# First products begun on half their input, and an expert stage whose weight slots join in another order, with a sixth in layer 1

## Chip, core and metric

One NeuronCore of a Trainium2 chip runs the whole program; all tensors are float32. The metric is device time in microseconds (us), the median over runs. A profiled execution is a separate run of the same kernel whose trace is read here.

## What is computed

Two transformer blocks in sequence over 256 latent tokens with 1024 channels, beside 256 context tokens. The first block has two layers. Each layer is a mixer and an expert feed-forward:

```
h = modulate(rms_norm(x));  z = h @ w_in                  # 256 latent + 256 context rows
y = gated sum of (fourier mix, global attention, window attention) @ w_out
x = x + g1 * y
h = modulate(rms_norm(x));  aff = softmax(h @ w_router)   # 16 experts
top_aff, top_idx = top_k(aff.T, 32)                       # each expert takes its 32 tokens
a, u = h[top_idx] @ w_gate_e, h[top_idx] @ w_up_e         # per expert, 1024 x 1024 each
x = x + g2 * scatter_add((silu(a) * u) @ w_down_e * top_aff)
```

In layer 0 latent and context tokens both go through the experts (64 rows per expert), in layer 1 the latent tokens alone (32 rows). The experts' matrices are 3 x 4 MB for each of 16 experts, 201 MB a layer. The second block has one layer: a hybrid mixer (gated linear attention and a state-space part), then a dense SwiGLU feed-forward of width 2816.

## The kernel before

Five engine programs are written by hand and kept in order by counting semaphores. Each engine waits for its signals in program order, so what stands behind a waiting instruction waits too. `due(name, n)` adds n to an engine's own count of a semaphore and returns the value to wait for.

**Weights** come through a ring of `RING = 4` slots of 16 KB per partition (2 MB each). One load fills one slot: half of a 1024 x 1024 expert matrix, or 512 columns of another one. The sync engine's program (SP) issues all loads in the order in which TensorE will use them. `Slots` (L118) gives both programs the same turn: `take` hands out the slot at the head of the list and puts it at the end. `load` (L1843) waits until the former holder of its slot was read: `release` counts whole jobs, and `release_half` signals when the first half of a matrix was read.

In the expert stage a fifth slot, number `RING`, joins. It lies in the SBUF area `arena` at 12288, where layer-wide tables (`pick`, `pick_g`) stand earlier in the layer, so its first load waits for `picks_turned`, the job number behind the last transposed pick (L1779, L1850).

**Order of the expert stage's loads**, numbered from 0: gate and up of expert 0, first halves (0, 1), second halves (2, 3); then for each expert e the four of expert e+1, and the two halves of down e (so 4 to 7 belong to expert 1, 8 and 9 to down 0). There are 96. With `slots.add(RING)` the fifth slot is appended behind the four of the ring: load 4 goes into it, and every later load n takes the slot of load n-5.

**Order of TensorE's work in the expert stage** (`experts`, L1689): router logits and their turns, places, then `gather` (L1598): for each of 8 k, products of `xn2` and the one-hot `pick` that collect the chosen rows as columns of `xgT`. VectorE modulates and copies the even k (L2339), ScalarE the odd ones (L2704). Then `turn_picks` (transposes for the later scatter, copied by VectorE, L2348), a wait for `xg_ready` (L2343, behind `xgT_done` of ScalarE, L2738), then `gate_up(0, 0)`, `gate_up(0, 1)`. `gate_up(e, half)` (L1724) is 32 products of 512 columns over four k. `turn_hidden`, `down` and, every fourth expert, `scatter` follow.

**PSUM** is two pools of four banks: pool D is read by VectorE, pool A by ScalarE. `bank(pool)` waits for the bank's reader of four jobs ago.

**First products.** Four places start with normalised rows `xn` that TensorE transposes (`turn_half`, L1419) and VectorE (even k) and ScalarE (odd k) modulate into `hT`, four k at a time with a signal each, `hT_ready_dve` (L2222) and `hT_ready_act` (L2653). They are the two mixers of the first block, the second block, and its feed-forward. TensorE waits for both signals of each engine (`wait_stream`, L1431; also L400 and L642) ahead of the first product that reads them. A product over the inner dimension runs through k = 0 to 7.

**Start of the program** (L1811 to L1831): the modulation steps `mod_step` (products with `w_ada`, L1370; turned by L1386) stand between transposes of `xn` for both streams.

## Time and profile before

| what | us |
|---|---|
| runs | 2429.85 median of 3 (2420.85, 2429.85, 2430.94) |
| the profiled execution's own time | 2430.49 |
| its span, first to last instruction | 2428.7 |
| TensorE busy | 2152.5 (89%) |
| VectorE busy | 689.0 (28%) |
| ScalarE busy | 390.6 (16%) |
| mean granted TensorE clock | 0.937 |
| bytes read | 589 MB, 243 GB/s over the span |

The stages of the first block: layer 0's experts run from about 573 to 1090 us of the span, layer 1's from about 1399 to 1905 us; in between stand the mixers; the second block runs from 1918 us to the end. The own time is 1.8 us longer than the span. A product of 512 float32 columns shows as two records.

### The profile page before, as it was taken

The numbers are of one execution on the slowest core, as the hardware profiler recorded it, in microseconds if no ns is written. First come the engines' busy times: TensorE is split into PE (matmuls) and PEld (weight loads), VectorE is DVE, ScalarE is ACT, GpSimd is POOL, SyncE is SP. The second block draws the span as 40 slices with busy tenths as digits, with TensorE's granted clock in tenths as the row PEclk, the third lists the DMA queues.
The fourth block names the chain that finished last, engine by engine and source line by source line (L and its number), as shares of the span: only waits on it lengthen the run. The fifth ranks groups of instructions, "written<-read, shape, count | busy, mean of one in ns | idle before, by whom it ended". The sixth has DMA issues, their size and how long they took to land.

```text
span 2428.7 us, 21162 instructions
## 1 busy us (share of the span) xinstructions
PE 2152.5 (89%) x8446; PEld 1021.1 (42%) x8446; DVE 689.0 (28%) x1642; ACT 390.6 (16%) x811; POOL 0.2 (0%) x4
## 2 busy tenths in 40 slices
PE   6989999998889898989899967888888798989998
PEld 3445444444323332324544432222222345648873
DVE  2266111045112121223631231121111358740001
ACT  2045100012100000002430110010000214441000
POOL 0000000000000000000000000000000000000000
PEclk8999899999989998989999989899999999889999
DMA  9139523111799999992384339999999620113442
GB/s 352 69 113 364 209 87 95 69 69 70 320 428 428 429 429 426 429 415 85 134 329 143 139 158 422 429 429 429 429 425 429 234 80 25 70 62 112 148 156 78
DMA packets 106411, 591.62 MB, mean 244 GB/s; under 512 B 8151, under 2 KB 12071, under 8 KB 81611
## 3 DMA queue, kind: packets, MB, share of 16 engines
q1 hardware_dynamic: 102720, 585.34, 59.9%
q10 hardware_dynamic: 3595, 4.95, 0.6%
q8 instruction: 67, 1.10, 0.2%
q14 instruction: 29, 0.24, 0.0%
HBM read 589.22 MB, written 1.05 MB: 243 GB/s over the span
## 4 chain that ended last, share of the span: by engine, by line
PE 73%; DMA 17%; DVE 5%; ACT 2%; issue 2%; DVEq 0%; SPq 0%; ACTq 0%
PE bank L1404 23%; PE bank L1733 18%; DMA weight_ring<-in_w_up_e 13%; PE bank L654 6%; PE bank L1353 4%; PE bank L408 3%; PE bank L673 3%; PE bank L1760 3%; PE bank L1370 3%; DMA arena<-in_w_up_e 2%; DMA weight_ring<-in_w_ada 2%; PE bank L1604 2%; PE bank L1721 2%; PE bank L1682 1%; PE bank L469 1%
## 5 line engine op out<-in xcount | busy, mean ns | idle before, releaser
L1733 PE MATMUL bank<-weight_ring,arena 128*64 128x512 f32 (+1 forms) x1664 | 504.0, 652 | 113.0 <-DMA weight_ring<-in_w_up_e 89.5
L1404 PE MATMUL bank<-weight_ring,arena 128*128 128x512 f32 (+1 forms) x1360 | 581.6, 590 | 6.8 <-DVE small L2222 4.1
L1404 PEld LDWEIGHTS bank<-weight_ring,arena 128*128 128x128 f32 x1360 | 261.0, 193 | 322.0 <-issue 310.3
L1733 PEld LDWEIGHTS bank<-weight_ring,arena 128*64 128x64 f32 (+1 forms) x1664 | 146.1, 134 | 378.5 <-issue 372.9
L1733 PE MATMUL bank<-arena 128*64 128x512 f32 (+1 forms) x384 | 185.6, 640 | 19.8 <-DMA weight_ring<-in_w_up_e 15.3
L1760 PE MATMUL bank<-weight_ring,arena 128*64 128x512 f32 (+1 forms) x800 | 177.9, 593 | 0.4 <-DMA weight_ring<-in_w_down_e 0.4
L1353 PE MATMUL bank<-const,arena 128*128 128x128 f32 (+4 forms) x808 | 121.8, 305 | 62.9 <-DVE arena L2075 10.2
L2745 ACT ACTIVATE arena<-bank 64x512 f32<-64x512 f32 (+1 forms) x64 | 37.7, 589 | 768.0 <-PE bank L1733 767.8
L654 PE MATMUL bank<-arena,weight_ring 128*128 128x256 f32 x704 | 153.9, 382 | 2.2 <-DVE small L2222 2.2
L1353 PEld LDWEIGHTS bank<-const,arena 128*128 128x128 f32 (+4 forms) x808 | 106.3, 178 | 114.3 <-issue 65.8
L654 PEld LDWEIGHTS bank<-arena,weight_ring 128*128 128x128 f32 x704 | 134.9, 192 | 21.1 <-DVE small L2222 2.5
L2428 DVE TENSOR_TENSOR arena<-bank,arena 32x512 f32<-32x512 f32 x96 | 65.8, 686 | 183.2 <-PE bank L1760 181.0
L2413 DVE COPY arena<-bank 128x512 f32<-128x512 f32 (+1 forms) x32 | 17.9, 558 | 339.9 <-PE bank L1353 339.8
L2404 DVE TENSOR_TENSOR arena<-bank,arena 64x512 f32<-64x512 f32 (+1 forms) x64 | 44.1, 689 | 230.4 <-ACT arena L2745 229.0
L1760 PEld LDWEIGHTS bank<-weight_ring,arena 128*64 128x64 f32 (+1 forms) x800 | 53.9, 123 | 118.9 <-issue 113.7
L1370 PE MATMUL bank<-weight_ring,silu_c 128*32 128x512 f32 x576 | 73.2, 654 | 15.8 <-DMA weight_ring<-in_w_ada 15.8
L1733 PEld LDWEIGHTS bank<-arena 128*64 128x64 f32 (+1 forms) x384 | 48.8, 132 | 78.4 <-issue 72.0
L408 PE MATMUL bank<-arena,weight_ring 128*128 128x512 f32 (+3 forms) x192 | 76.1, 558 | 1.8 <-DVE small L2222 1.8
L673 PE MATMUL bank<-weight_ring,arena 128*128 128x512 f32 x176 | 75.8, 593 | 1.1 <-DVE arena L1102 1.1
L2155 DVE TENSOR_TENSOR arena<-bank,arena 128x512 f32<-128x512 f32 x24 | 16.6, 692 | 192.5 <-PE bank L1404 192.5
L2630 ACT ACTIVATE arena<-bank 128x512 f32<-128x512 f32 x36 | 21.5, 597 | 274.8 <-PE bank L1404 274.8
L1760 PE MATMUL bank<-arena 128*64 128x512 f32 (+1 forms) x224 | 52.4, 610 | 4.5 <-DVE arena L2413 4.0
(368 smaller groups left out, 1569.2 us busy)
## 6 DMA issues: line engine op xcount, KB each, us to landing
weight_ring<-in_w_gate_e SPq DMA_DIRECT2D x52, 2048.0 KB, 15.4
weight_ring<-in_w_up_e SPq DMA_DIRECT2D x52, 2048.0 KB, 12.3
weight_ring<-in_w_down_e SPq DMA_DIRECT2D x50, 2048.0 KB, 12.6
weight_ring<-in_w_ada SPq DMA_DIRECT2D x24, 2048.0 KB, 12.2
weight_ring<-in_w_in SPq DMA_DIRECT2D x23, 2048.0 KB, 9.9
arena<-in_w_down_e SPq DMA_DIRECT2D x14, 2048.0 KB, 14.6
arena<-in_w_gate_e SPq DMA_DIRECT2D x12, 2048.0 KB, 15.7
arena<-in_w_up_e SPq DMA_DIRECT2D x12, 2048.0 KB, 14.8
```

The source lines that it names most:

```text
L408: mm = pe.matmul(b[0:m, 0:n], slot_view(r)[:, k, c0:c0 + m], hT[:, k, 0:n], start=(k == 0), stop=(k == KD - 1))
L654: mm = pe.matmul(b[:, n * SEQ:n * SEQ + SEQ], slot_view(r)[:, k, blk * P:blk * P + P], h3T[:, k, :], start=(k == 0), stop=(k == KD - 1))
L673: mm = pe.matmul(bs[t][:, :], ffT[:, k, t * P:t * P + P], slot_view(r)[:, k - k0, :], start=(k == 0), stop=(k == FB - 1))
L1353: return pe.transpose(dst, src, ident[0:src.shape[0], 0:src.shape[0]])
L1370: mm = pe.matmul(b[at:at + 32, :], silu_pad[:, col:col + 32], wide(r)[:, k, n * 512:n * 512 + 512], start=(k == 0), stop=(k == KH - 1))
L1404: mm = pe.matmul(b[:, 0:c1 - c0], lhs[:, k, t * P:t * P + P], slot_view(r)[:, k, c0:c1], start=(k == 0), stop=(k == ks - 1))
L1604: mm = pe.matmul(b[:, :], xn2[:, t, every8(k)], pick[:, t, :], start=(t == 2 * s), stop=(t == 2 * s + 1))
L1721: pe.matmul(b[:, :], putT[:, t, g, :], out_g[:, stream_of(t), n * 512:n * 512 + 512], start=True, stop=True).then_inc(S("fullD"), 1)
L1733: mm = pe.matmul(banks_[n][c:c + R, :], xgT[:, KH * half + k, e, 0:R], wide(r)[:, k, n * 512:n * 512 + 512], start=(half == 0 and k == 0), ...
L1760: mm = pe.matmul(b[64 * n:64 * n + R, :], hidT[:, KH * half + k, 0:R], wide(r)[:, k, n * 512:n * 512 + 512], start=(half == 0 and k == 0), ...
L2404: dve.tensor_tensor(hid[0:R, n * 512:n * 512 + 512], b[64:64 + R, :], silu_g[0:R, n, :], ALU.mult).then_inc(S("hid_ready"), 1)
L2428: dve.tensor_tensor(out_g[rows_, s, n * 512:n * 512 + 512], b[64 * n + CAP * s:64 * n + CAP * s + CAP, :], gate2_b[rows_, s, n * 512:n * 5 ...
```

## The change

It has seven parts. (1) At the four places named above, the first product waits for one signal of each engine, does k = 0 to 3, waits for the other, and does k = 4 to 7. (2) At the start, the transposes of the second stream stand behind the third modulation step instead of ahead of it. (3) In both expert stages five k are gathered, then `gate_up(0, 0)` runs behind a wait for the fourth k's copy alone, then the last three k are gathered, the picks are turned (all by pool A, copied by ScalarE), and `gate_up(0, 1)` follows. (4) `weigh_picks` moves between VectorE's third and fourth copies. (5) In layer 0 the extra slot takes load 6 instead of load 4, and may be filled once the picks are turned. (6) In layer 1 there are two extra slots, for loads 4 and 5, which may be filled once `m_sum` is complete and turned; tables of layer 1 move to other places in `arena` for that. (7) The wait ahead of the scatter's first use covers ScalarE's copies of the picks. In the diff stand in turn: the slots, the tables, the second block (its feed-forward's first product is changed alike), the mixer, TensorE's expert stage, the start of the program, SP's load, and the expert stage of VectorE and of ScalarE.

```diff
 class Slots:
     def take(self):
+        if self.taken in self.joins:
+            self.turn.insert(0, self.joins.pop(self.taken))
         r = self.turn.pop(0)
         self.turn.append(r)
...
-    def add(self, r):
-        self.turn.append(r)
+    def add(self, r, takes):
+        self.joins[self.taken + takes] = r
...
-        h2T = (area(4096, KD, SEQ), area(16384, KD, SEQ))
-        xgT = area(0, KD, E, 64)
-        pick = area(12288, TILES, 512)
-        pick_g = area(14336, TILES, 512)
+        h2T = ((area(4096, KD, SEQ), area(16384, KD, SEQ)), (area(18432, KD, SEQ),))
+        xgT = (area(0, KD, E, 64), area(0, KD, E, CAP))
+        pick = (area(12288, TILES, 512), area(10240, 2, 512))
+        pick_g = (area(14336, TILES, 512), area(11264, 2, 512))
...
-        gate2_b = area(18432, 2, D)
+        gate2_b = (area(18432, 2, D), area(17408, 1, D))
...
-            return ring[:, r, :] if r < RING else area(12288, SLOT)
+            return ring[:, r, :] if r < RING else area((12288, 4096)[r - RING], SLOT)
+        def extra_slots(l):
+            return (RING,) if l == 0 else (RING, RING + 1)
...
-            pe.wait_ge(S("hT_ready_dve"), due("hT_ready_dve", 2))
-            pe.wait_ge(S("hT_ready_act"), due("hT_ready_act", 6))
+            pe.wait_ge(S("hT_ready_act"), due("hT_ready_act", 4))
...
                 for k in range(KD):
+                    if first and k % KH == 0:
+                        pe.wait_ge(S("hT_ready_dve"), due("hT_ready_dve"))
+                        pe.wait_ge(S("hT_ready_act"), due("hT_ready_act"))
                     mm = pe.matmul(b[0:m, 0:n], slot_view(r)[:, k, c0:c0 + m], hT[:, k, 0:n], start=(k == 0), stop=(k == KD - 1))
...
-                wait_stream()
                 pe.wait_ge(S(f"slot_landed{weights[0]}"), due(f"slot_landed{weights[0]}", 16))
-                in_proj(0, 0)
+                b = bank("D")
+                for half in range(2):
+                    wait_half_stream()
+                    dense_half(b, 0, weights[0], hT, half)
...
                 turn_streams(m_sum, list(own))
+                if l:
+                    extra_free[1, RING] = ("m_ready", 2)
+                    extra_free[1, RING + 1] = ("fullA", T.n["freeA"])
...
                 if l == 0:
-                    turn_picks(0, "A")
-                    put_copied = T.n["freeA"]
+                    turn_picks(0, 0, "A")
                 turn_places(last, bank("D"))
                 pe.wait_ge(S("pick_ready"), due("pick_ready"))
-                gather(last, range(KD), "DA")
-                turn_picks(last, "D")
+                for k in range(5):
+                    pool = "DA"[k % 2]
+                    gather(l, last, k, bank(pool), pool)
+                    if k == 3:
+                        low_act = T.n["freeA"]
...
-                picks_turned.append(T.n["freeD"])
-                slots.add(RING)
-                pe.wait_ge(S("xg_ready"), due("xg_ready"))
-                if l == 0:
-                    pe.wait_ge(S("freeA"), POOL + put_copied)
+                late = bank("D")
                 pair = (next_bank(), next_bank())
                 gate_up_jobs[l, 0] = T.n["freeD"] - 1
+                for n, r in enumerate(extra_slots(l)):
+                    slots.add(r, 4 + n if l else 6)
+                pe.wait_ge(S("freeA"), POOL + low_act)
                 gate_up(0, 0, pair)
+                for k in range(5, KD):
+                    gather(l, last, k, late if k == 6 else bank("A"), "DA"[k % 2])
+                high_act = T.n["freeA"]
+                turn_picks(l, last, "A")
+                put_copied = T.n["freeA"]
+                if l == 0:
+                    extra_free[0, RING] = ("fullA", put_copied)
+                pe.wait_ge(S("freeD"), POOL + gate_up_jobs[l, 0] - 1)
+                pe.wait_ge(S("freeA"), POOL + high_act)
                 gate_up(0, 1, pair)
...
+                    if e == 4:
+                        pe.wait_ge(S("freeA"), POOL + put_copied)
...
             turn_half(xn, 0, "A", 1)
+            pe.wait_ge(S("silu_c_ready"), due("silu_c_ready", 4))
+            mod_step(*EARLY_STEPS[2])
             turn_half(xn, 1, "A", 1)
-            pe.wait_ge(S("silu_c_ready"), due("silu_c_ready", 4))
-            for step in EARLY_STEPS[2:]:
-                mod_step(*step)
+            mod_step(*EARLY_STEPS[3])
...
-                elif r == RING:
-                    sp.wait_ge(S("fullD"), picks_turned[0])
+                elif r >= RING:
+                    signal, jobs = extra_free[layer[0], r]
+                    sp.wait_ge(S(signal), jobs)
...
-                take_places(last)
-                weigh_picks(last)
+                take_places(l, last)
                 for k in range(0, KD, 2):
+                    if k == 6:
+                        weigh_picks(l, last)
...
-                dve.wait_ge(S("xgT_done"), due("xgT_done"))
-                dve.memset(flag, 0.0).then_inc(S("xg_ready"), 1)
...
-                    dve.tensor_copy(putT[:, t, :, :], b[:, :].rearrange("p (g i) -> p g i", g=4)).then_inc(S("freeD"), 1)
...
                 take_gathered(l, last, range(1, KD, 2))
-                act.activation(flag_a, zero, ACT.Copy).then_inc(S("xgT_done"), 1)
+                take_picks(last)
```

## Rows read from the trace of the kernel before

**Rows 1.** The page's chain that ended last, by engine.
```profile
PE 73%; DMA 17%; DVE 5%; ACT 2%; issue 2%; DVEq 0%; SPq 0%; ACTq 0%
```

**Rows 2.** What the DMA engines moved in the page's 40 slices of 60.7 us.
```profile
GB/s 352 69 113 364 209 87 95 69 69 70 320 428 428 429 429 426 429 415 85 134 329 143 139 158 422 429 429 429 429 425 429 234 80 25 70 62 112 148 156 78
```

**Rows 3.** Waits of TensorE, longest in total: us, times, longest.
```profile
PE bank L1733 <- DMA weight_ring<-in_w_up_e: 104.8, 29, 6.3
```

**Rows 4.** Windows: us, busy of PE, PEld, DVE, ACT, POOL, clock, DMA share, GB/s.
```profile
640.00:740.00 100.00, 84.33 (x368) 30.12 (x366) 15.92 (x35) 3.67 (x7) 0.00 (x0) 0.91 1.01 429
1460.00:1860.00 400.00, 335.53 (x1442) 105.35 (x1440) 56.59 (x140) 22.65 (x39) 0.00 (x0) 0.92 1.01 427
```

**Rows 5.** Timeline of the start: start, us, engine, line, operation.
```profile
29.60 0.94 ACT L2801 ACTIVATE silu_c<-vecs 128x8 f32<-128x8 f32 x4
30.01 3.67 PE L1353 MATMUL bank<-const,arena 128*128 128x128 f32 x16
33.61 4.36 PE L1370 MATMUL bank<-weight_ring,silu_c 128*32 128x512 f32 x32
...
43.70 0.06 DVE L2222 MEMSET small<- 128x1 f32 x1
...
45.24 8.86 PE L1404 MATMUL bank<-weight_ring,arena 128*128 128x512 f32 x16 [1.98 <-DVE small L2222]
```

**Rows 6.** Timeline at the other three first products: first half's signal, then the product.
```profile
1104.56 0.06 DVE L2222 MEMSET small<- 128x1 f32 x1
...
1105.96 8.83 PE L1404 MATMUL bank<-weight_ring,arena 128*128 128x512 f32 x16 [2.08 <-DVE small L2222]
...
1922.83 0.06 DVE L2222 MEMSET small<- 128x1 f32 x1
...
1924.23 6.28 PE L408 MATMUL bank<-arena,weight_ring 128*128 128x512 f32 x14 [1.84 <-DVE small L2222]
...
2190.30 0.06 DVE L2222 MEMSET small<- 128x1 f32 x1
...
2191.70 4.54 PE L654 MATMUL bank<-arena,weight_ring 128*128 128x256 f32 x12 [2.24 <-DVE small L2222]
```

**Rows 7.** Timeline where layer 0's experts begin.
```profile
612.13 0.81 DVE L2339 TENSOR_SCALAR arena<-bank,mod_cols 128x512 f32<-128x512 f32 x1 [2.63 <-PE bank L1604]
...
618.07 0.33 SPq L1852 DMA_DIRECT2D arena<-in_w_gate_e  x1
...
618.88 13.95 PE L1733 MATMUL bank<-weight_ring,arena 128*64 128x512 f32 x64 [0.84 <-DVE small L2343]
...
626.01 0.33 SPq L1852 DMA_DIRECT2D weight_ring<-in_w_up_e  x1
```

**Rows 8.** Timeline where layer 1's experts begin.
```profile
1398.74 0.33 SPq L1852 DMA_DIRECT2D weight_ring<-in_w_gate_e  x1
...
1432.86 0.78 ACT L2704 ACTIVATE arena<-bank,mod_cols 128x512 f32<-128x512 f32 x1 [2.66 <-PE bank L1604]
...
1434.59 0.81 DVE L2339 TENSOR_SCALAR arena<-bank,mod_cols 128x512 f32<-128x512 f32 x1 [2.62 <-PE bank L1604]
...
1440.53 0.33 SPq L1852 DMA_DIRECT2D arena<-in_w_gate_e  x1
...
1440.98 13.93 PE L1733 MATMUL bank<-weight_ring,arena 128*32 128x512 f32 x64 [0.48 <-DVE small L2343]
...
1448.09 0.33 SPq L1852 DMA_DIRECT2D weight_ring<-in_w_up_e  x1
```

**Rows 9.** Windows: first product, starts of both layers' experts; columns as in rows 4.
```profile
45.00:49.00 4.00, 3.76 (x5) 1.71 (x6) 0.04 (x1) 2.80 (x7) 0.00 (x0) 0.53 1.04 389
...
624.00:628.00 4.00, 4.00 (x22) 1.35 (x20) 0.00 (x0) 0.00 (x0) 0.00 (x0) 1.00 0.46 123
...
1411.00:1440.00 29.00, 19.61 (x46) 11.63 (x46) 13.04 (x32) 5.32 (x8) 0.00 (x0) 0.71 0.00 1
...
1448.00:1452.00 4.00, 4.00 (x22) 1.05 (x18) 0.00 (x0) 0.00 (x0) 0.00 (x0) 1.00 0.75 254
```

More of the change, by code:

```diff
@@ L295, in build @@
         gate_up_jobs = {}
[L296 removed]
+        extra_free = {}
         probs_turned_jobs = {}
@@ L1807, in experts @@
                 scatter(3)
-                slots.drop(RING)
+                for r in extra_slots(l):
+                    slots.drop(r)
             pe.wait_ge(S("ident_landed"), 16)
@@ L1841, in _ @@
             slots = Slots()
+            layer = [0]
             def load(*pieces):
@@ L1902, in load_gate_up @@
                             load((lambda r: wide(r), halves[name][e, half]))
-                slots.add(RING)
-                slots.holder.pop(RING, None)
+                layer[0] = l
+                for n, r in enumerate(extra_slots(l)):
+                    slots.add(r, 4 + n if l else 6)
+                    slots.holder.pop(r, None)
                 load_gate_up(0)
```

90 lines of the change are left out of this document (44 added, 46 removed).

## The prediction

> **What bounds the kernel now.** I read the page's chain first: three quarters are TensorE, and the next share is DMA [rows 1]. The slices say where: in slices 11 to 18 and 25 to 32 the traffic stands flat near 428 GB/s, and elsewhere it is mostly far below [rows 2]. Those two plateaus are the expert stages. TensorE's longest wait in total is there, for up matrices [rows 3]. Two windows inside the plateaus show a DMA share of full and 427 to 429 GB/s, with TensorE 84% busy [rows 4]. So inside an expert stage loads set the pace: one load of 2.097 MB takes 2097/428 = 4.9 us, and 96 take 470 us. Outside, TensorE sets it, with short waits for the other two engines. In both kinds of stage, everything later hangs on what went before by counting signals, so I take a shift of a stage's start as a shift of the end, unless stated.
>
> A DMA plateau can only move if it begins sooner. Before layer 1's experts the engines stand still for 29 us at 1 GB/s [rows 9], because no slot is free. From issue to first data 1.5 us pass: load 5 of layer 1 is issued at 1448.09 [rows 8], and the window from 1448 to 1452 moved 254 x 4 = 1016 KB, 2.4 us at full rate, so it began at 1449.6 [rows 9].
>
> **First products in halves.** Removed is the wait for the second half's signals. VectorE's signal for the first half starts at 43.70, the product at 45.24 [rows 5]. After the second signal TensorE needs 0.1 to 0.2 us, so the product can begin at 43.9: 1.3 us. The other three places each show 1.40 us between the first signal and the product [rows 6], less 0.06 for the signal and 0.12 to wake: 1.2 us each, 3.6 together. Added are two waits in each; the four k of the first half take at least 4 x 0.4 x 2 halves of a float32 product, some 3 us, so the second signal (1.3 us after the first) is there in time. In the feed-forward a product has 256 columns and the four k take about 1.7 us; still enough. The transposes of stream 1 and VectorE's next copies are queued behind the product and move with it.
>
> **Start.** The second stream's transposes (half of the 3.67 us at 30.01, thus 1.8) stand ahead of the step at 33.61, whose conditions are ready at 30.54 [rows 5]. Behind the step they fall into a wait in which VectorE turns the step's result into a row, 1.7 us. Gain 1.6 us. Least 0 (if the weights' arrival takes over); most 3.6, if with the idle time gone the first product (8.86 us, of which rival (b) shows 2 to be the clock's) also runs at full clock.
>
> **Layer 0's experts.** Before: load 4 went out at 618.07, the products began at 618.88 and freed two slots at 626.01, so load 5's data began at 627.5 [rows 7]. The window from 624 to 628 moved only 123 GB/s: the plateau begins after it [rows 9]. After: k = 4 is gathered when its copy starts, 612.13; the fourth k's copy (ScalarE) is over by then. `gate_up(0, 0)` runs from 612.1 for 7.1 us (618.88 to 626.01) to 619.2, and loads 4 and 5 follow one another from 620.7. Load 5's data begins at 620.7 + 4.9 = 625.6: 1.9 us sooner. The extra slot, now third in line, is wanted at 630.5 and free once the three late gathers and the picks are done, 6.2 us after 619.2: 625.4. The next two slots come free at 632.4, data at 633.9, and loads 4 to 6 last until 635.4. No hole. Bounds: 0, since load 4 itself is now 0.9 us later, to 3.
>
> **Layer 1's experts.** Before: load 4 at 1440.53, load 5's data from 1449.6, so load 8's from 1449.6 + 3 x 4.9 = 1464.3; its slot was freed in time, when the 13.93 us of products from 1440.98 were over [rows 8]. After: loads 2 and 3 still go out at 1398.74, and 4 and 5 directly behind them, because both extra slots' conditions were met long before; all four land by 1422, in the idle stretch. `gate_up(0, 0)` starts after k = 4 (copy at 1434.59; the one of k = 3 is over at 1433.64), at 1434.6, and frees two slots at 1441.7; their data runs from 1443.2 to 1453.0. Then three gathers of 1.7 us (distance of the copies of k = 3 and 4) and the picks' turn, together 6.2, and `gate_up(0, 1)`, 6.9: slots free at 1454.8, load 8's data from 1456.3. The plateau is interrupted from 1453.0 to 1456.3, but load 8 is 8.0 us sooner. From there on loads 4 and 5 are already there, so `gate_up(1, 0)` frees two more slots at 1462, before the data of 8 and 9 ends at 1466. Bounds: 1.7, if the extra slots were not filled early; 11.3, if the hole closed.
>
> **Six slots in the steady part** I cost at nothing. The window of 400 us in layer 1 already shows 427 against 429 at best [rows 4]. The Trainium skill, in DMA: Bandwidth & Descriptors, section "Where 436 GB/s comes from", puts the ceiling of the 16 ports at 435 GB/s; by that figure 191 MB would take 439 us instead of 446, an estimate of 7 us to gain that the row of 429 at best does not grant.
>
> **Edits at no cost.** VectorE's two picks' copies (1.4 us) go to ScalarE, which is otherwise idle until the first `silu`; `weigh_picks` (1.4 us) hides beside `gate_up(0, 0)`, seven us long, and if that cover went, the turn of the picks and then `gate_up(0, 1)` would be late. `late` takes one bank of pool D out of turn; its reader of four jobs ago is done. On SP's queue the extra loads stand behind the last load of expert 0 only, and nothing else waits behind them that was free before. In layer 0 the next layer's first load takes a slot freed half a `down` later, 3.5 us; the plateau still has two loads ahead of it.
>
> **Sum.** 1.6 + 1.3 + 3.6 + 1.9 + 8.0 = 16.4 us. The profiled execution took 2430.49 with a span of 2428.7, and lies 0.6 us over the median of the runs: 2430.5 - 16.4 = 2414.1, rounded to 2414.0, 0.67% under it. About 0.5%, 12.1 us, is what a measurement here tells from no change; the three runs themselves span 10 us.
>
> **Rivals.**
> (a) The sixth slot does not do what it says: SP, strictly in order, finds an extra slot's condition late (a table still in use), so loads 4 and 5 of layer 1 wait like those of layer 0. For it: both conditions are counts that I worked out from the order alone. Against: the area's last use is long past at 1398.74. Then layer 1 gives 1.7 instead of 8.0: 2420.4.
> (b) The clock eats what the halves give. At 45.24 and 1105.96 sixteen records take 8.9 us [rows 5, 6]; fourteen take 6.28 at 1924.23 [rows 6], 0.43 each, so 6.9 would do. The granted clock was 0.53 from 45 to 49 us [rows 9], the level of 1.2 GHz for most of it, after waits for the other engines. If the rise to 2.4 GHz stays where it is in time, work begun 1.2 us sooner counts half, which costs 0.6 at each of four places: 2416.5. The Trainium skill's rule (TensorE: Matmul & The Clock Gate, "Why this matters for your kernels") is that the clock follows sustained work, by which the rise would move along and cost nothing; but it also says that the moment varies.
> (c) More than forecast: the hole in layer 1 closes or the small stalls of its plateau go (8.0 becomes 11.3, and 2 us of 446 by 427 against 429), and the start gains its 3.6: 2430.5 - 16.4 - 3.3 - 2 - 2 = 2406.8.
> (d) Slower: with a sixth load in flight, all into the same partitions that engines read, layer 1's plateau carries less. It decides below 191 MB / (446 + 16.4) = 412 GB/s, where all gains are gone; at 400 GB/s, 477 us against 446, the end is 2445. For it: the traffic is not always flat, as slice 18 with 415 shows [rows 2]. Against: the plateau with a fifth slot in `arena` runs at 427 to 429 already [rows 4].
>
> **Chances.** Forecast 0.55, (a) 0.17, (b) 0.12, (c) 0.10, (d) 0.06. Of the forecast's 0.55, 0.06 falls within 0.5% by the scatter of runs; of (b) half; (a) is within. Faster by over 0.5%: 0.49 + 0.06 + 0.10, some 0.65. Slower by over 0.5%: 0.04 of (d). Within: 0.31. The range reaches up past (a), 2425, and down past (c), 2405; (d) and the tails are left out.
>
> **What would show it.** Right: TensorE's first products at 43.9 minus 1.6 and, each shifted, 1.2 us behind the first signal; an `arena` load issued right after the second load near 1399, two of them in layer 1, and 1 GB/s only from about 1422; a hole of some 3 us in the traffic near 1453; end of layer 1's experts 14 to 16 us sooner. Wrong: a wait of TensorE ahead of `gate_up(0, 0)` or `gate_up(0, 1)`, a rate in layer 1's plateau below 420, an SP wait between loads 3 and 4 of layer 1, or a wait taking the place of the removed ones in the attention of layer 0.

## The result, and the profile after

The changed kernel takes 2406.27 us (median of 5 runs, 2403.93 to 2410.18), beside 2424.76 us for the kernel before in the same session (5 runs, 2420.85 to 2430.94). The ratio is 0.9922, with a 95% interval from 0.9901 to 0.9942. The forecast was 2414.0, in a range of 2405 to 2425, and faster: the sign and the range hold, the range by 1.3 us at its lower end, and the gain is 18.5 us by the medians instead of 16.4. The profiled execution took 2406.17 us, with a span of 2404.3 us, and a mean granted clock of 0.942 after 0.937.

The page of the changed kernel: the chain by engine, and the traffic in 40 slices of 60.1 us.

```profile
PE 71%; DMA 19%; DVE 6%; ACT 2%; issue 2%; SPq 0%; DVEq 0%; ACTq 0%
GB/s 356 70 109 363 220 88 88 79 70 70 292 430 428 430 428 427 427 420 143 128 329 156 140 210 395 430 429 430 430 429 430 234 74 32 71 60 116 156 151 79
```

The bounds are the same as in [rows 1] and [rows 2]: TensorE outside the plateaus, DMA inside. The plateaus stand at the same height; the slice ahead of layer 1's rises to 210 from 158, and the first of its own is at 395.

Layer 1's experts in the timeline, beside [rows 8]:

```profile
1387.76 0.33 SPq L1888 DMA_DIRECT2D weight_ring<-in_w_gate_e  x1
1388.13 0.43 SPq L1888 DMA_DIRECT2D weight_ring<-in_w_up_e  x1
1388.61 0.43 SPq L1888 DMA_DIRECT2D arena<-in_w_gate_e  x1
1389.08 0.49 SPq L1888 DMA_DIRECT2D arena<-in_w_up_e  x1
...
1423.44 7.06 PE L1756 MATMUL bank<-weight_ring,arena 128*32 128x512 f32 x32
...
1430.54 0.33 SPq L1888 DMA_DIRECT2D weight_ring<-in_w_gate_e  x1
...
1436.07 0.78 ACT L2735 ACTIVATE arena<-bank,mod_cols 128x512 f32<-128x512 f32 x1 [2.66 <-PE bank L1622]
...
1436.95 7.06 PE L1756 MATMUL bank<-weight_ring,arena 128*32 128x512 f32 x32
...
1444.04 0.80 SPq L1888 DMA_DIRECT2D weight_ring<-in_w_down_e  x2
...
1446.23 3.20 PE L1756 MATMUL bank<-arena 128*32 128x512 f32 x14 [2.22 <-DVE small L2437]
```

Loads 2 to 5 are issued within 1.3 us of one another, two into `arena`; load 6 goes out 42.8 us after load 2, load 8 after 56.3 us. One call of `gate_up` is 16 products of 512 columns, each shown as two records, hence x32 (the 32 products of the text on the kernel before are these records). The windows (columns as in [rows 4]) show what the engines moved in the idle stretch, in the hole and in a second dip, and the steady part:

```profile
1393.00:1409.00 16.00, 7.36 (x35) 3.33 (x33) 8.45 (x29) 5.37 (x10) 0.00 (x0) 0.50 0.99 425
1411.00:1423.00 12.00, 10.50 (x20) 6.29 (x20) 3.01 (x4) 1.55 (x2) 0.00 (x0) 0.76 0.00 1
1441.00:1445.00 4.00, 3.01 (x15) 0.72 (x10) 0.00 (x0) 1.75 (x2) 0.00 (x0) 1.00 0.17 74
1453.00:1459.00 6.00, 6.00 (x34) 2.30 (x34) 0.48 (x2) 0.00 (x0) 0.00 (x0) 1.00 0.93 362
1460.00:1860.00 400.00, 337.03 (x1446) 105.65 (x1444) 58.72 (x144) 23.08 (x39) 0.00 (x0) 0.92 1.01 429
```

Layer 0's experts, beside [rows 7]: the first half-product, loads 4, 6 and 7.

```profile
611.24 7.09 PE L1756 MATMUL bank<-weight_ring,arena 128*64 128x512 f32 x32
...
618.37 0.33 SPq L1888 DMA_DIRECT2D weight_ring<-in_w_gate_e  x1
...
624.71 0.33 SPq L1888 DMA_DIRECT2D arena<-in_w_gate_e  x1
...
631.90 0.33 SPq L1888 DMA_DIRECT2D weight_ring<-in_w_up_e  x1
```

The first products, beside [rows 5, 6]: program start, mixer 1, block 2, feed-forward.

```profile
30.13 1.97 PE L1364 MATMUL bank<-const,arena 128*128 128x128 f32 x8
...
32.03 4.82 PE L1381 MATMUL bank<-weight_ring,silu_c 128*32 128x512 f32 x32
...
42.74 9.77 PE L1571 MATMUL bank<-weight_ring,arena 128*128 128x512 f32 x16 [1.04 <-ACT small L2684]
...
1097.00 0.06 DVE L2260 MEMSET small<- 128x1 f32 x1
...
1097.31 1.95 PE L1571 MATMUL bank<-weight_ring,arena 128*128 128x512 f32 x4 [1.18 <-DVE small L2260]
...
1905.08 2.38 PE L418 MATMUL bank<-arena,weight_ring 128*128 128x512 f32 x5 [0.76 <-DVE small L2260]
...
2169.08 2.18 PE L665 MATMUL bank<-arena,weight_ring 128*128 128x256 f32 x9 [0.96 <-DVE small L2260]
```

Each stands 0.31 us behind the first half's signal (1097.00 to 1097.31), where it stood 1.40 us behind it.

**Where the time went.** I cut each trace at eight events: the issue of load 2 in each layer's expert stage, the end of its last `down`, the first products of mixer 1, block 2 and the feed-forward, and the end. Lengths are differences of their starts, in us. "Front" is the experiment with the halves and the swap alone (below).

| stretch | before | front | after | after - before | forecast |
|---|---|---|---|---|---|
| start to layer 0's load 2 | 572.8 | 567.4 | 572.0 | -0.8 | -2.9 |
| experts 0 | 511.4 | 510.6 | 508.8 | -2.6 | -1.9 |
| to mixer 1's first product | 21.8 | 20.6 | 16.5 | -5.3 | -1.2 |
| mixer 1, to layer 1's load 2 | 292.8 | 293.5 | 290.4 | -2.4 | 0 |
| experts 1 | 504.8 | 505.2 | 497.7 | -7.1 | -8.0 |
| to block 2's first product | 20.7 | 19.6 | 19.6 | -1.1 | -1.2 |
| to the feed-forward's | 267.5 | 259.8 | 264.0 | -3.5 | -1.2 |
| feed-forward | 237.0 | 235.3 | 235.3 | -1.7 | 0 |

The stretches sum to 24.4 us, the difference of the spans; the medians differ by less, 18.5, since the profiled execution of before was 5.7 us over its median (2430.49 against 2424.76). Two stretches vary from profile to profile of nearly the same work, mostly with the granted clock: the first from 567.4 to 573.1 us (mean clock 0.96 in the shortest and 0.95 in the longest), and block 2 from 259.4 to 268.2 us. Their differences say nothing about the change. The other stretches mostly repeat within 0.3 us where the work is the same, and are what the experiments are read by. The exceptions: with the halves and the swap alone, two profiles (the second in the last experiment) gave 510.6 and 511.4 us for layer 0's experts, and 293.5 and 290.4 us for mixer 1.

Two rows are far larger than my steps for them: the way to mixer 1, and mixer 1 itself, together 7.7 us where 1.2 was forecast. There the clock differs, not the work. The same sixteen records (eight products) of the last scatter, before, then after:

```profile
1087.28 10.09 PE L1721 MATMUL bank<-arena 128*128 128x512 f32 x16 [3.16 <-DVE small L2432]
```
```profile
1083.97 7.13 PE L1744 MATMUL bank<-arena 128*128 128x512 f32 x16 [3.16 <-DVE small L2463]
```

And the windows from there to mixer 1's first product, before and after (columns as in [rows 4]); the clock, third from the end, is 0.77 and 1.00:

```profile
1084.00:1106.00 22.00, 13.70 (x35) 7.30 (x33) 13.09 (x30) 7.67 (x16) 0.00 (x0) 0.77 0.53 203
```
```profile
1081.00:1097.00 16.00, 9.10 (x32) 4.69 (x32) 11.75 (x26) 6.95 (x15) 0.00 (x0) 1.00 0.78 296
```

### The profile page after: what moved, and what is told of

Read it like the earlier page. It is cut to its first block, busy times and chain, and to the rows that moved or that the text cites. A ratio compares the mean times of both kernels' runs of the same rounds, so it can differ in the third digit from the quotient of the medians.

```text
span 2404.3 us, 21163 instructions
## 1 busy us (share of the span) xinstructions
PE 2141.6 (89%) x8446; PEld 1016.1 (42%) x8446; DVE 686.1 (29%) x1636; ACT 392.3 (16%) x813; POOL 0.2 (0%) x4
## 4 chain that ended last, share of the span: by engine, by line
PE 71%; DMA 19%; DVE 6%; ACT 2%; issue 2%; SPq 0%; DVEq 0%; ACTq 0%
PE bank L1415 23%; PE bank L1756 16%; DMA arena<-in_w_up_e 12%; PE bank L665 6%; DMA weight_ring<-in_w_up_e 5%; PE bank L1364 3%; PE bank L418 3%; PE bank L684 3%; PE bank L1381 3%; PE bank L1783 2%; PE bank L1622 2%; PE bank L1571 2%; DMA weight_ring<-in_w_ada 1%; PE bank L1744 1%; PE bank L1700 1%
## 5 line engine op out<-in xcount | busy, mean ns | idle before, releaser
L1415 PE MATMUL bank<-weight_ring,arena 128*128 128x512 f32 (+1 forms) x1328 | 559.8, 584 | 2.7 <-DVE small L2212 1.9
L1756 PE MATMUL bank<-weight_ring,arena 128*64 128x512 f32 (+1 forms) x1376 | 375.5, 630 | 49.6 <-DMA weight_ring<-in_w_up_e 33.7
L1415 PEld LDWEIGHTS bank<-weight_ring,arena 128*128 128x128 f32 x1328 | 252.3, 190 | 305.9 <-issue 298.9
L1756 PE MATMUL bank<-arena 128*32 128x512 f32 (+1 forms) x672 | 226.4, 688 | 74.7 <-DMA arena<-in_w_up_e 55.7
L1756 PEld LDWEIGHTS bank<-weight_ring,arena 128*64 128x64 f32 (+1 forms) x1376 | 115.6, 133 | 247.2 <-issue 238.5
L1783 PE MATMUL bank<-weight_ring,arena 128*32 128x512 f32 (+1 forms) x896 | 200.0, 597 | 3.1 <-DVE arena L2444 2.9
L1364 PE MATMUL bank<-const,arena 128*128 128x128 f32 (+4 forms) x808 | 119.9, 301 | 63.1 <-DVE arena L2113 10.2
L1756 PEld LDWEIGHTS bank<-arena 128*32 128x32 f32 (+1 forms) x672 | 63.4, 134 | 199.5 <-issue 187.9
L1783 PEld LDWEIGHTS bank<-weight_ring,arena 128*32 128x32 f32 (+1 forms) x896 | 61.5, 123 | 135.7 <-issue 128.9
L418 PEld LDWEIGHTS bank<-arena,weight_ring 128*128 128x128 f32 (+2 forms) x192 | 33.5, 176 | 43.0 <-issue 41.0
```

What stands on the lines that cost most here:

```text
L418: mm = pe.matmul(b[0:m, 0:n], slot_view(r)[:, k, c0:c0 + m], hT[:, k, 0:n], start=(k == 0), stop=(k == KD - 1))
L1364: return pe.transpose(dst, src, ident[0:src.shape[0], 0:src.shape[0]])
L1415: mm = pe.matmul(b[:, 0:c1 - c0], lhs[:, k, t * P:t * P + P], slot_view(r)[:, k, c0:c1], start=(k == 0), stop=(k == ks - 1))
L1756: mm = pe.matmul(banks_[n][c:c + R, :], xgT[l][:, KH * half + k, e, 0:R], wide(r)[:, k, n * 512:n * 512 + 512], start=(half == 0 and k == ...
L1783: mm = pe.matmul(b[64 * n:64 * n + R, :], hidT[:, KH * half + k, 0:R], wide(r)[:, k, n * 512:n * 512 + 512], start=(half == 0 and k == 0), ...
```

## The experiments

Twelve kernels ran. Unless said otherwise each is the changed kernel with the edit shown. "Before" beside them had medians of 2420.95 to 2423.45 us, each of 13 or 15 runs.

**The changed kernel once more**, for a scale.

> The changed kernel once more, unedited, to separate its gain from the luck of the clock. My sum, corrected by what the trace of after shows stage by stage, is 14 to 16 us under the kernel before (ratio 0.9935 to 0.9945). If the extra 3 to 5 us that the first comparison gave belong to the change, the ratio is 0.992 again; if the clock gave them, it lies nearer 0.994, and the mean granted clock of each run tells long runs from short ones.

Measured: 2406.32 us (6 runs), before 2423.08, ratio 0.9919 (0.9904 to 0.9933). The stretches repeat: 508.7, 16.5, 290.4, 497.8, 19.6 and 235.3 us; the first is 568.0 and block 2 takes 267.7.

**The halves and the swap alone**, on the kernel before.

```diff
+                    if first and k % KH == 0:
+                        pe.wait_ge(S("hT_ready_dve"), due("hT_ready_dve"))
+                        pe.wait_ge(S("hT_ready_act"), due("hT_ready_act"))
...
+            mod_step(*EARLY_STEPS[2])
             turn_half(xn, 1, "A", 1)
```

> The kernel before with only parts 1 and 2: first products in halves at the four places, and the second stream's transposes behind the third modulation step. Expert stages as before. My sum: 1.6 + 1.3 + 3.6 = 6.5 us less, ratio 0.9973. The clock rival: 3 to 4.5 us less, with the first product ending 1.6 us sooner though it begins 2.5 us sooner, and 1.1 to 1.2 us at each of the other three.

Measured: 2416.76 us (8 runs), ratio 0.9970 (0.9956 to 0.9985), 6.3 us by the medians and 7.3 by the ratio. The way to block 2 is 1.1 us shorter and the one to mixer 1 1.2; both expert stages are within 0.8 us of before, and the clock is as low behind layer 0's:

```profile
1078.00:1098.00 20.00, 13.36 (x32) 7.20 (x32) 11.59 (x25) 7.46 (x15) 0.00 (x0) 0.74 0.58 223
```

So the halves and the swap give about the 6.5 us that were forecast, and the 4.1 us more on the way to mixer 1 (20.6 to 16.5) come with the rest of the change.

**One extra slot in layer 1**, five instead of six.

```diff
-            return (RING,) if l == 0 else (RING, RING + 1)
+            return (RING,)
```

> The changed kernel with one extra slot in layer 1 in place of two (it takes load 4, early). If the sixth slot is what makes load 8 early: loads 5 and 6 follow gate_up(0, 0), loads 7 and 8 gate_up(0, 1), so load 8's data begins one load later, 4.9 us less the hole, and the end is 4 to 5 us later than the changed kernel's; the hole near 1443 us stays at 3.5 us. If the sixth slot is worth nothing (DMA at its limit anyway), no difference.

Measured: 2406.91 us (6 runs, 2403.75 to 2413.99), ratio 0.9930 (0.9913 to 0.9947). The profiled run was the slowest of them; in it layer 1's experts take 507.9 us, 10.2 more than after. The hole ends as it did, 56.3 us after load 2 by the issues, but with load 7 instead of load 8, so every later load comes one load later, the 4.9 us that were foreseen. The rest is lost in the steady part, 424 GB/s over 400 us instead of 429, which is 4.7 us:

```profile
1460.00:1860.00 400.00, 331.68 (x1422) 101.65 (x1418) 58.72 (x144) 23.08 (x39) 0.00 (x0) 0.92 1.00 424
```

One of its stalls in the timeline: a half-product that ran in part at half clock took 9.33 instead of 7.06 us and released its slots that much later.

```profile
1535.80 9.33 PE L1756 MATMUL bank<-weight_ring,arena 128*32 128x512 f32 x32 [6.25 <-DMA weight_ring<-in_w_up_e]
...
1545.16 0.33 SPq L1888 DMA_DIRECT2D weight_ring<-in_w_down_e  x1
```

From 1540 to 1550 us the engines moved 400 GB/s there. The changed kernel has an equally slow half-product, and the traffic holds around its end:

```profile
1528.31 9.32 PE L1756 MATMUL bank<-arena 128*32 128x512 f32 x32 [5.86 <-DMA arena<-in_w_up_e]
...
1532.50:1542.50 10.00, 10.00 (x52) 3.46 (x50) 0.48 (x2) 0.00 (x0) 0.00 (x0) 0.98 1.00 426
```

In this profile the sixth slot is thus worth about 5 us in the hole and up to 5 in the steady part. But 424 is not what five slots carry in general: the kernel before, with five, shows 427 over its window [rows 4]. The medians don't bear that size out: the two intervals overlap, and by the ratios five slots cost 2.7 us more, within the scatter. That a second slot helps is shown in the one profile; by how much over many runs stays open.

**All gathers and picks ahead of the first half-product**, in both layers.

```diff
-                pe.wait_ge(S("freeA"), POOL + low_act)
-                gate_up(0, 0, pair)
                 for k in range(5, KD):
...
                 pe.wait_ge(S("freeA"), POOL + high_act)
+                gate_up(0, 0, pair)
                 gate_up(0, 1, pair)
```

> The changed kernel with both halves of expert 0's products behind all eight gathers and the turned picks, as before; slots and their turn as in the changed kernel. TensorE does the same work until the end of gate_up(0, 1). By my reckoning layer 0 loses 6.5 us (loads 4 and 5 wait for gate_up(0, 0), the extra slot stands third), layer 1 only 2.9 us (loads 6 and 7 go out at 1437 instead of 1430.5, no hole): 9 to 10 us later than the changed kernel. If the order of the products were the whole gain of layer 1, it would lose 7 us there alone.

Measured: 2409.17 us (6 runs, 2401.48 to 2413.59), ratio 0.9931 (0.9912 to 0.9950). Layer 0's experts take 514.3 us, 5.5 more; layer 1's 499.1, 1.4 more. That is 6.9 us where 9 to 10 were expected, and of it the medians show 2.9 (2409.17 against 2406.32), in runs that scatter by 12. For layer 1 it says what carries the gain: with the products in the old order, the two early slots alone bring 504.8 down to 499.1.

**Layer 0's extra slot first in line again.**

```diff
-                    slots.add(r, 4 + n if l else 6)
+                    slots.add(r, 4 + n)
```

> The changed kernel with layer 0's extra slot first in line (load 4) instead of third (load 6); it still becomes free only when the picks are turned, now at about 624 us. SP works in order, so load 4 waits there with loads 5 and 6 behind it, though their slots are free 6.3 us sooner. My theory: layer 0's stage is 6 us longer than the changed kernel's, layer 1 the same; 6 us at the end. The rival, that DMA catches up since the plateau has slack, gives no difference. Granted-clock luck of the parts outside the expert stages moves the end by some us either way, so the stage's own length decides.

Measured: 2413.17 us (8 runs), ratio 0.9958 (0.9943 to 0.9974). Layer 0's experts take 515.4 us, 6.6 more, and the median is 6.9 above that of the changed kernel's repeat; layer 1's are unchanged. The queue of SP shows the mechanism: load 4 waits for the picks, and 5 and 6, whose slots are free, behind it.

```profile
625.74 0.33 SPq L1888 DMA_DIRECT2D arena<-in_w_gate_e  x1
626.11 0.43 SPq L1888 DMA_DIRECT2D weight_ring<-in_w_up_e  x1
626.59 0.43 SPq L1888 DMA_DIRECT2D weight_ring<-in_w_gate_e  x1
```

Load 4 is issued 52.7 us after load 2 (at 573.07), where after it was 46.3 (618.37, load 2 at 572.03).

**Layer 1's two extra slots joined late**, for loads 6 and 7, freed by the picks.

```diff
-                    slots.add(r, 4 + n if l else 6)
+                    slots.add(r, 6 + n)
...
-                if l == 0:
-                    extra_free[0, RING] = ("fullA", put_copied)
+                for r in extra_slots(l):
+                    extra_free[l, r] = ("fullA", put_copied)
```

> The changed kernel with layer 1's two extra slots filled late: free when the picks are turned, in line for loads 6 and 7. Six slots as in the changed kernel, but nothing is loaded into them in the idle stretch. If early filling is the gain: loads 4 and 5 follow gate_up(0, 0), load 8's data begins after 4 to 7, 6 us later than in the changed kernel, and layer 1's stage is 5 to 6 us longer (503.5 against 497.8). If six slots in flight by themselves are the gain (no small stalls in the plateau), the stage stays within 2 us of the changed kernel's.

Measured: 2408.42 us (6 runs, 2401.70 to 2415.30), ratio 0.9932 (0.9911 to 0.9953). Layer 1's experts take 504.2 us, 6.5 more, and thus what they took before the change (504.8). The profiled run was the slowest of the six, and by the medians this kernel is only 2.1 us over the changed kernel's repeat and 4.0 to 4.3 over the two that follow, in the same session. In the profile, six slots that are filled late win 0.7 us: what wins is that two loads more land in the idle stretch. The experiment with the gathers first says the same from the other side (early slots without the new order, 499.1).

**Layer 1's picks turned after `gate_up(1, 0)`**, to let `gate_up(0, 1)` begin sooner; and the same **with `silu`'s table loaded early**.

```diff
+                    if l and e == 0:
+                        turn_picks(l, last, "A")
...
+                act.activation(flag_a, zero, ACT.Silu).then_inc(S("act_step"), 1)
```

> A version meant to beat the changed kernel: in layer 1 the picks are turned behind gate_up(1, 0) instead of ahead of gate_up(0, 1), and copied behind expert 0's silu; weighed picks of layer 1 lie at 18432. Load 8's slot comes free 1.0 us sooner, and since the traffic stands still there (1442 to 1445.5), all of it should reach the end of layer 1's stage: 496.8 instead of 497.8. A rival: the next two loads, which wait for gate_up(1, 0) and its banks, become the bound, and nothing is won.

> As e7, and ScalarE computes one silu of a single column ahead of each layer's first expert, so that the table load of 1.28 us, which now stands behind the first pair of products, is over before it. gate_up(1, 0) waits 2.2 us for banks that the hidden rows free, and the traffic dips from 1455 to 1458 because of it; 1.3 us less wait closes this dip of about 1 us. Expected for layer 1's stage: 495.8 to 496.2. Rival: the table is loaded again anyway (Copy or the scale of the gathered columns evicts it), then as e7.

Measured: 2404.38 and 2404.10 us (6 runs each), ratios 0.9916 (0.9899 to 0.9934) and 0.9916 (0.9900 to 0.9931). Layer 1's experts take 497.5 and 497.8 us: nothing gained. The turn of the picks, 1.04 us, had stood beside the wait for ScalarE's copy of gather 7 (the row at 1436.07 above, over at 1436.85; the half-product follows at 1436.95). Without it TensorE waits for the same copy, and load 8 is issued 56.3 us after load 2 as before. I had costed the picks as if they stood alone on the path.

The early table did what it should at its own place: load 10 went out 64.3 instead of 65.6 us after load 2, and the second dip closed. The window that stands to load 2 as 1453 to 1459 did after:

```profile
1451.50:1457.50 6.00, 6.00 (x33) 2.33 (x34) 0.48 (x2) 0.87 (x2) 0.00 (x0) 1.00 1.01 425
```

Yet the stage took 497.8 us, and not the 495.8 to 496.2 that were expected, so the microsecond of traffic in that dip is not a microsecond of the stage.

**Layer 0's products in the old order and its extra slot first in line**, both of these edits undone. It is not wholly the old stage: the picks are still copied by ScalarE, `weigh_picks` keeps its new place, and the wait for `xg_ready` is gone.

```diff
-                pe.wait_ge(S("freeA"), POOL + low_act)
-                gate_up(0, 0, pair)
+                if l:
+                    pe.wait_ge(S("freeA"), POOL + low_act)
+                    gate_up(0, 0, pair)
...
+                if l == 0:
+                    gate_up(0, 0, pair)
                 gate_up(0, 1, pair)
...
-                    slots.add(r, 4 + n if l else 6)
+                    slots.add(r, 4 + n)
```

> The changed kernel with layer 0's experts as before (all eight gathers and the picks ahead of the first gate_up, the extra slot first in line); layer 1, the halves and the swap as changed. The profiles leave open where 5 us between the end of layer 0's experts and mixer 1's first product come from: 21.8 and 20.6 us in the two profiles with the old expert stages (TensorE's granted clock fell to half from 2 to 9 us and from 16 to 19 us after the stage's end), 16.5 us in all profiles with changed stages (no such stretch until 83 us after it), also where only the gathers or only the slot's place were undone. Theory (the clock's stretches stand where the work of layer 0's expert stage puts them, and either of its two changes moves them): with both undone the stage of layer 0 takes 511 to 515 us, the stretch to mixer 1 is 20.6 to 21.8 us again, mixer 1 293 us, layer 1's stage 497.7 us, the median 2406.3 + 2.3 + 5 + 2.5 = 2415 to 2417 us. Rival (it hangs on something else that the change moved, such as places in the arena, or on chance): the stretch stays 16.5 us, mixer 1 290.4 us, and the median is 2408.5 to 2411 us.

Measured: 2407.71 us (10 runs, 2405.00 to 2416.63), ratio 0.9937 (0.9916 to 0.9957). Two things come out. First, layer 0's experts take 509.2 us, only 0.4 more than with both edits, though either one alone costs 5.5 or 6.6. The window of 30 us that begins 50 us after load 2 is at 400 GB/s here and at 424 after (rows below), 1.7 us of loads; of this 0.4 reaches the end of the stage, whose last 40 us had a clock of 0.91 here and 0.87 after. The last of its 96 loads is issued 490.0 us after load 2, where it is 489.3 after, and 491.1 and 491.9 in the two profiles of the halves and the swap alone. Of the 1.8 to 2.6 us by which it comes sooner, the two edits hold 0.7; the rest came with the other edits in layer 0 or is scatter.

```profile
620.00:650.00 30.00, 27.39 (x124) 10.52 (x122) 3.53 (x9) 3.64 (x5) 0.00 (x0) 0.94 0.96 400
1039.00:1079.00 40.00, 33.10 (x144) 12.74 (x144) 7.17 (x16) 2.67 (x4) 0.00 (x0) 0.91 1.01 417
1079.00:1095.00 16.00, 9.13 (x34) 4.69 (x32) 11.67 (x25) 6.77 (x14) 0.00 (x0) 1.00 0.82 311
```
```profile
622.00:652.00 30.00, 27.32 (x123) 11.24 (x123) 3.80 (x9) 5.61 (x8) 0.00 (x0) 0.94 1.01 424
1041.00:1081.00 40.00, 33.80 (x144) 11.99 (x144) 6.72 (x17) 2.67 (x4) 0.00 (x0) 0.87 1.01 416
```

Second, the clock behind the stage stays at 1.00 and the way to mixer 1 at 16.5 us: the theory that the order of the products or the slot's place sets it has fallen; the parts of the change that this kernel keeps in layer 0 are not tested by it. Mixer 1 itself takes 293.5 us again, and a later profile of the kernel with the halves and the swap shows 290.4 (below): its 3 us belong neither to the order of layer 0 nor to the change as a whole.

**`gate_up(0, 1)` in halves too**: on top of the early table it waits for the copy of gather 7 only ahead of its last step.

```diff
                     for k in range(KH):
+                        if last_copied is not None and k == KH - 1:
+                            pe.wait_ge(S("freeA"), last_copied)
...
-                pe.wait_ge(S("freeA"), POOL + high_act)
-                gate_up(0, 1, pair)
+                pe.wait_ge(S("freeA"), POOL + high_act - 1)
+                gate_up(0, 1, pair, POOL + high_act)
```

> The kernel with late picks and the early Silu table, and gate_up(0, 1) waits for ScalarE's copy of gather 7 only ahead of its last step, k = 7. In the two kernels before it nothing was won since gate_up(0, 1) stood behind that copy anyway: it began 0.97 us after gather 7 had ended, 49.2 us after layer 1's first release, with or without the picks ahead of it. Now load 8 of layer 1 is issued 55.3 instead of 56.3 us after load 2. Theory (every us by which loads come earlier while the DMA queues stand still is a us of the stage): layer 1's stage takes 496.6 to 496.9 instead of 497.8 us, the median 2403 us. Rival (what is won at the hole is lost again in the next 60 us, as it seems to have been with the early table: the dip of 1 us at 68 to 72 us after load 2 had gone, and as much more was missing at 90 to 120 us): 497.5 to 497.9 us, the median 2404.2 us.

Measured: 2398.89 us (6 runs, 2397.34 to 2412.50), ratio 0.9904 (0.9876 to 0.9932). Layer 1's experts take 495.7 us, 2.1 less.

```profile
1386.92 0.33 SPq L1894 DMA_DIRECT2D weight_ring<-in_w_gate_e  x1
...
1435.07 7.06 PE L1758 MATMUL bank<-weight_ring,arena 128*32 128x512 f32 x32
1442.17 0.80 SPq L1894 DMA_DIRECT2D weight_ring<-in_w_down_e  x2
1443.08 7.06 PE L1758 MATMUL bank<-arena 128*32 128x512 f32 x32 [0.95 <-DVE small L2443]
```

Load 8 goes out 55.25 us after load 2, 1.0 sooner, as expected. Its median is the lowest found. Its stage gains 1 us more than that us, and its median 5 us on the kernel without the edit, but the two intervals (0.9876 to 0.9932, 0.9900 to 0.9931) overlap; the second us and the rest are not traced to a cause.

**The last turn of layer 0 doubled**, on the changed kernel and on the one with the halves and the swap, to shift the end of the stage by a us.

```diff
-                    for k in range(KD):
+                    for k in (*range(KD), *range(KD)) if l == 0 and e == E - 1 else range(KD):
                         mm = turn(b[:, k * 64:k * 64 + R], hid[0:R, every8(k)])
```

> The changed kernel, and the hidden rows of layer 0's last expert are turned twice (16 instead of 8 small matmuls, about 1.1 us more on TensorE ahead of the last down); nothing else. The run before this showed that the 4 to 5 us between the end of layer 0's experts and mixer 1 don't hang on how layer 0's expert stage is ordered: with both of its changes undone the stretch was 16.5 us all the same, so that theory has fallen. What is left: TensorE's half-clock stretches happen to fall, after the stage, on the scatter and the norm in the old kernel (10.2 us of them there) and beside them in the new one (none). Theory (a matter of alignment, within a us or two): the extra us brings them back, the stretch from the last down's end to mixer 1 takes about 20.6 us and has 7 to 10 us at half clock; the median is 2406.3 + 1 + 4 = 2411 us. Rival (the clock is kept for a cause that stands far from this place): 16.5 us, no half clock, layer 0's stage 509.8 instead of 508.8 us, the median 2407.4 us.

> The kernel before with the halves and the swap alone, and the same doubling of the last turn in layer 0. Theory (alignment, within a us or two): one us is enough to move the half-clock stretches off the scatter and the norm, 16.5 instead of 20.6 us from the last down's end to mixer 1, and the median is 2416.8 + 1 - 4 = 2414 us. Rival: 20.6 us as in the kernel without the doubling, 10 us of it at half clock, the stage of layer 0 511.7 instead of 510.6 us, the median 2417.8 us. If this kernel stays at 20.6 and the changed one at 16.5 us, the place of the stretches is firm against 1 us and is set earlier in the kernel.

Measured: 2402.56 us (4 runs), ratio 0.9932 (0.9916 to 0.9949), and 2416.52 us (10 runs, 2409.05 to 2421.69), ratio 0.9970 (0.9951 to 0.9989). The ways to mixer 1 are 16.5 and 20.8 us, as without the doubling. But layer 0's stage ended at 508.9 and 511.4 us: the longer turn lay beside VectorE's additions for the expert before it,

```profile
1066.60 1.98 PE L1364 MATMUL bank<-const,arena 64*128 64x64 f32 x16
1066.79 2.85 DVE L2459 TENSOR_TENSOR arena<-bank,arena 32x512 f32<-32x512 f32 x4 [5.38 <-PE bank L1783]
1069.70 0.06 DVE L2463 MEMSET small<- 128x1 f32 x1
1069.80 0.69 DVE L2444 COPY arena<-bank 128x512 f32<-128x512 f32 x1
```

and the copy that the last `down` needs started only at 1069.80, behind those. Hardly anything was shifted in the changed kernel, and the 0.9 us in the other one is no more than the kernel before shows without the doubling (511.4), so the pair doesn't test how firm the place is. What it adds is two more profiles: the clock behind the stage repeats in both, and mixer 1 took 290.4 us in the kernel with the halves and the swap, where it had taken 293.5 in the first profile of that kernel.

## Why the prediction was right

**Start (1.6) and mixer 0's halves (1.3).** The transposes take 1.97 us in place of 3.67, the step begins at 32.03 instead of 33.61, 1.6 sooner, and the first product 2.5 sooner, at 42.74. But it takes 9.77 instead of 8.86 us, so that 1.6 of the 2.9 arrive (54.10 to 52.51). This is rival (b)'s mechanism at the one place out of four where it showed: the clock rose later in the work. What of the 1.6 is left 530 us later can't be told from the clock's scatter.

**The three other halves (3.6).** 1.1 us each, from the rows above (1.40 to 0.31 behind the first signal). Rival (b) failed at them: the clock was full in the first 4 us of each, also in mixer 1 and the feed-forward, where it had been 0.61 and 0.57 before. The first two rows are of after, the third of before:

```profile
1905.00:1909.00 4.00, 3.92 (x9) 1.82 (x10) 2.51 (x5) 0.00 (x0) 0.00 (x0) 1.00 0.01 4
2169.00:2173.00 4.00, 3.92 (x18) 3.51 (x19) 1.01 (x3) 0.00 (x0) 0.00 (x0) 1.00 0.54 195
```
```profile
2192.00:2196.00 4.00, 4.00 (x12) 3.22 (x11) 0.00 (x0) 0.00 (x0) 0.00 (x0) 0.57 0.12 42
```

That makes the last stretch of the table 1.7 us shorter, and it is so in every profile with the halves, the one with the halves and the swap alone too: a halved wait won more than itself there.

**Layer 0's experts (1.9).** The events stood where they were put: `gate_up(0, 0)` 6.9 us sooner by load 2's issue, load 4 issued at 46.3, the extra slot free at 624.71, ahead of 631.90. The stage is 2.6 us shorter than before, 1.8 than with the halves alone; undoing it costs 0.4. The step holds as 1.7 us of earlier traffic, and its worth at the stage's end as 0.4 to 2.6; that the clock in the last experts makes the difference is my reading, and not shown. What I had not said is that its two edits are worth nothing singly: each undone alone costs more than both together. And by the last load's issue (489.3 us after load 2, 490.0 with both undone, 491.1 or more without the rest) most of what the stage gained did not hang on them, but on the edits around them, which I had given no price, or on scatter.

**Layer 1's experts (8.0).** 7.1 us, and the mechanism is the one forecast. Rival (a) is out: the `arena` loads are issued at 1388.61 and 1389.08. The idle stretch, the first half-product and load 8 stand as forecast (load 8 at 56.1 us after load 2 by my steps, 56.3 in the trace). One thing was missing from my step, a wait for PSUM. I had `gate_up(1, 0)` free two slots 63.3 us after load 2 and the trace has load 10's issue at 65.6, since it waited 2.22 us for its banks, which VectorE frees only when `silu`, with its table load of 1.28 us, is done. The traffic dips there from 1453 to 1459, 6 x (428 - 362)/428 = 0.9 us, just what the stage lacks. But the experiment with the early table closed this dip and left the stage at 497.8, so where the missing us went stays open. The experiments price the parts, each from one profile: both slots early without the new order, 499.1; the new order with the slots late, 504.2; one early slot instead of two, 507.9, of which 4.9 us are the load that comes later and the rest stalls in the steady part.

**Six slots in the steady part (0).** 429 GB/s instead of 427 over 400 us [rows 4] is 1.9 us of traffic, part of rival (c). Rival (d), a lower rate, is out. The Trainium skill's ceiling of 435 GB/s (DMA: Bandwidth & Descriptors, "Where 436 GB/s comes from") isn't reached with six slots either: the best windows of 10 and 400 us read here show 433 and 429.

**What was not in any step: the clock behind layer 0's experts.** 4.1 us on the way to mixer 1 (20.6 to 16.5 beside the kernel with the same halves), and 2.4 us in mixer 1 in this pair of profiles, which came and went in both families (293.5 and 290.4 us each). On the way to mixer 1, all eleven profiles of the changed kernel and of its relatives show 16.5 us, all three of the kernel before, with or without the halves, show 20.6 to 21.8. It isn't bound to the order of layer 0's products, to the place of its extra slot, or to the extra slots of layer 1 (five, early or late). Not tested are the copies of the picks by ScalarE, the place of `weigh_picks`, the dropped waits and the tables' new places, nor is alignment ruled out: the last half-clock stretch inside the stage ends 4.5 to 4.8 us ahead of its end in the three profiles with the long way, and 5.2 to 5.6 in the eleven with the short one. Its cause stays open; that it will be there in each execution isn't shown either, since only one run of each kernel was profiled, and three of the ten runs of the last kernel, with a clock of 0.944 to 0.946, took 2409 to 2410 us, 6 to 7 under its median. The Trainium skill (TensorE: Matmul & The Clock Gate, "Why this matters for your kernels") advises to leave no idle gaps between bursts; the same gap of 3.16 us stands ahead of the scatter in both kernels, at half clock behind it in one and at full clock in the other, so that rule alone doesn't tell them apart.

**The base.** I put the sum against a profiled execution that lay 0.6 us over the median of three runs. Over all later runs the kernel's median is 2421 to 2425, and that execution lay 6 to 10 us over it. From 2424.76 my sum would have given 2408.4. So the time of 2414.0 was 7.7 us too high for two errors that go the same way, a base too high by 5.7 and a clock behind layer 0 that gave 4 unforeseen, and it is luck that the range still covered it: its lower end was drawn for rival (c), the hole closed, the start at full clock and 2 us in the plateau, of which only the last came. The gain of 16.4 came near 18.5 by luck of the other kind. The steps themselves gave some 14 (1.6 of 2.9, 3.3 of 3.6, about 1.9, 7.1 of 8.0), and the clock made up for what they lacked and more. The end of layer 1's experts, forecast 14 to 16 us sooner, came 18.0 sooner (1903.6 to 1885.5) for the same reason.

**Slips in the working.** The plateaus fill slices 12 to 18 and 25 to 31 [rows 2], not 11 and 32; and layer 0's load 4 comes 1.1 us later by the forecast's own steps (1.0 in the traces), not 0.9; rival (d)'s 412 GB/s is 413. None moves the sum.

## What to carry to other kernels

Where transfers bound a stage, find the time in which they stand idle ahead of it, and ask which buffer is free by then: two slots filled early won what six slots in flight alone didn't. A queue that runs in order must meet its slots in the order in which they come free, so a reordering of work and one of slots may be worth something only together; test them together and singly. And before a wait is shortened, look which second wait ends within a us of it: the picks hid a copy, and only the edit that split the wait for that copy shortened the stage (by 2.1 us, in one profile).

## What the runs showed of the hardware

- The granted clock's half stretches keep their place against a stage within a kernel, and decide several us: the same sixteen records took 10.09 and 7.13 us. The first 570 us and block 2 vary by 6 and 9 us between profiles of the same work there.
- Counted back at full rate, 1.4 to 1.5 us passed from an issue to the plateau's first data (load 6 of layer 1, issued at 1430.54: the window from 1429 to 1433 moved 111 GB/s, 1.0 us at full rate). The first packets of that load start at 1431.50, 0.96 us after the issue. The plateau carried 427 GB/s over 400 us with five slots before and 429 with six, and 424 in the one profile of the changed kernel with five.
- A half-product of 9.3 us, in part at half clock, was enough to break the plateau in that profile with five slots (400 GB/s over 10 us), and not with six (426).
